# Scoring both attention heads of a pair in one TensorE step, with the transposes grouped, in a hybrid conv/MLA block

## The chip, the cores and the metric

One core of one Trainium2 chip runs the whole program. The metric is the device time of one execution in microseconds; a shorter time is better. The engines of the core run side by side, each with its own queue of instructions in program order: TensorE (PE in the profile, with its weight loads as PEld), VectorE (DVE), ScalarE (ACT), GpSimd (POOL) and SyncE (SP), which issues the DMAs.

## The reference, cut to what matters

```python
D_MODEL, SEQ, CHUNK = 2048, 256, 64
N_HEADS, QK_NOPE, QK_ROPE, V_DIM = 8, 128, 64, 128
...
proj = rms_norm(x) @ w_in                  # u | gate_b | gate_c | c_q | c_kv | k_rope_raw
q  = (rms_norm(c_q)  @ w_uq).reshape(b, s, N_HEADS, QK_NOPE + QK_ROPE)
kv = (rms_norm(c_kv) @ w_ukv).reshape(b, s, N_HEADS, QK_NOPE + V_DIM)
q_rope, k_rope = apply_rope(q_rope), apply_rope(k_rope_raw)      # one k_rope for all heads
for start in range(0, 256, 128):           # two blocks of queries: keys 0..127, keys 0..255
    s = (einsum(q_nope[start:end], k_nope[:end]) + einsum(q_rope[start:end], k_rope[:end])) * scale
    s = where(visible, s, NEG_INF)
    p = softmax(s)
    o = einsum(p, v[:end])
y = concat(short_conv(...), group_rms_norm(o)) @ w_o
x = x + rms_norm(y)
x = x + rms_norm(square(relu(rms_norm(x) @ w_up)) @ w_down)      # d_ff = 8192
```

All inputs, weights and the output are float32. The score of a query and a key is the sum of a 128-long product (the "nope" part) and a 64-long product (the rotary part).

## The kernel before, in words

**The stream.** Every product with a weight matrix is made from a high and a low part of both operands, three matmuls for one (L593, L594, L595: high by high, low by high, high by low), 128x512 outputs for the most part. Two blocks of 128 tokens make six matmuls of one "step" ("mm" in the list of steps). Weights come in "quads" of four chunks of 128 rows (three for the q projection), 1 MB each, by DMA into four slots of `raw`. Two chunks are a half. ScalarE makes the high part of a half (L882, `split_hi`, 128x1024) once TensorE has used the half that was in its place, and VectorE then the low part (L1141, `split_lo`). There are four places for halves (`AHEAD = 4`): when half h has been used, half h+4 is split into its place.

**The order.** `plan()` (L74) writes by hand one list of steps, and every engine runs its own part of each step in that order. While the strips of the input projection that belong to the convolution, and then the output projection, stream through TensorE, a counter `sub` counts the steps, and `between(sub)` (L115) puts the small steps of attention and convolution between them. The eight heads are worked on as four pairs p = 0 to 3. Pair p starts at sub = 16 + 16p: four kv steps at `at` = 0, six steps of q at `at` = 4, and then the list in L131: kT at 6, qT at 7, qrT at 9, the scores of head 0 at 11 and of head 1 at 12, the transposes of the probabilities of head 0 at 13 and of head 1 at 15, the product with v at 18, and the norm and transposes of the output at 20 to 25. Pairs are 16 steps apart, so the kv step of pair p+1 is at `at` = 16 of pair p.

**The small steps on TensorE.** A transpose is a 128x128 matmul against `ident` (`transposes`, L598, L601), four in a row for kT (bank 4) and qT (bank 5), two for qrT, three for the probabilities of each head (bank 5 for head 0, bank 6 for head 1). A scores step (L770) makes, for one head, four float32 products: L783 with q and k transposed (contraction over 128 rows) and L785 with the rotary parts (contraction over 64 rows; head 0 uses partitions 0 to 63, head 1 partitions 64 to 127), first both for the 128 queries that see 128 keys, then both for the 128 queries that see 256 keys. The profile shows each such float32 product as two weight loads and two matmuls; below they are called its two passes. The results of head 0 lie in bank 6 of PSUM, of head 1 in bank 4.

**The other engines.** For a scores step VectorE masks with two memsets, takes the row maxima and scales them (L1246 to L1251); ScalarE then does two exponentials with row sums (L1007). For probsT, VectorE copies head 0's transposes out of bank 5 (L1258) and ScalarE head 1's out of bank 6 (L1014). The kv step of the next pair writes banks 4 and 5, so TensorE waits ahead of it (L662, L663):

```python
pe.wait_ge(probs_ready, 2 * z["p"])
pe.wait_ge(probsT0_ready, z["p"])
```

Of the kernel before, what the change touches and what calls it, by code (L numbers as in the profile page):

```python
# [33 lines left out]
P = 128  # L34
SEQ = 256
# [38 lines left out]
def plan():  # L74
# [40 lines left out]
    def between(sub):  # L115
        if sub == 7:
            steps.extend([("latT", 0, 0), ("latT", 1, 0), ("krT", 0, 0), ("latT", 2, 0)])
        if sub == 10:
            steps.extend([("latT", 3, 0), ("latT", 4, 0)])
        for p in range(PAIRS):  # L120
            at = sub - 16 - 16 * p
            if at == 0:
                n = quad("kv", p=p, nk=4, width=W)
                products(n)
                steps.append(("kv_out", p, n))
            if at == 4:
                for part in range(2):
                    n = quad("q", p=p, part=part, nk=3, width=QW)
                    products(n)
                steps.append(("q_out", p, n))  # L130
            for when, what, h in [(6, "kT", 0), (7, "qT", 0), (9, "qrT", 0), (11, "scores", 0),  # L131
                                  (12, "scores", 1), (13, "probsT", 0), (15, "probsT", 1), (18, "pv", 0),
                                  (20, "o_squares", 0), (21, "o_norm", 0), (25, "oT", 0)]:
                if at == when:
                    steps.append((what, p, h))
        for c in range(4):
            for half, t in [(0, 77 + 6 * c), (1, 98 + 4 * c)]:
                if sub == t:
                    steps.append(("convT", half, c))
                if sub == t + 2:  # L140
                    steps.append(("conv_square", half, c))
                if sub == t + 5:
                    steps.append(("conv_norm", half, c))
# [119 lines left out]
def hybrid_block(nc, t, out):  # L263
# [7 lines left out]
    with ExitStack() as ctx:  # L271
# [314 lines left out]
        def _(pe):  # L586
# [148 lines left out]
            def step(what, a, b):  # L735
# [4 lines left out]
                elif what == "mm_b1":  # L740
                    stream(a, b, [1])
                elif what == "latT":
                    pe.wait_ge(lat_ready, 1)
                    pe.wait_ge(ident_landed, 16)
                    if a >= 3:

                        pe.wait_ge(latT_lo_ready, a - 2)
                    transposes(LAT_BANK[a], [lat[:, tb, lat_cols(a, c):lat_cols(a, c) + P]
                                             for c in range(2) for tb in range(TB)]).then_inc(latT_filled, 1)
                elif what == "krT":  # L750
                    pe.wait_ge(kr_ready, 4)
                    transposes(6, [kr_rot[:, tb].rearrange("p e r -> p (e r)")
                                   for tb in range(TB)]).then_inc(krT_filled, 1)
                elif what == "kT":

                    pe.wait_ge(q_ready, a + 1)
                    pe.wait_ge(kv0_ready, a + 1)
                    pe.wait_ge(kv1_ready, a + 1)
                    transposes(4, [k_sb[:, tb, h] for h in range(2) for tb in range(TB)]).then_inc(kT_filled, 1)
                elif what == "qT":  # L760
                    pe.wait_ge(q_ready, a + 1)
                    transposes(5, [q_sb[:, tb, h * (NOPE + ROPE):h * (NOPE + ROPE) + NOPE]
                                   for h in range(2) for tb in range(TB)]).then_inc(qT_filled, 1)
                elif what == "qrT":
                    pe.wait_ge(q_rope_ready, 4 * (a + 1))

                    pe.wait_ge(kT_ready, a + 1)
                    transposes(4, [qr_rot[:, tb].rearrange("p e r -> p (e r)")
                                   for tb in range(TB)]).then_inc(qrT_filled, 1)
                elif what == "scores":  # L770
                    p, h = a, b
                    pe.wait_ge(kT_ready, p + 1)
                    pe.wait_ge(qT_ready, p + 1)

                    pe.wait_ge(qrT_ready, p + 1)

                    pe.wait_ge(krT_ready, 1)
                    if p and not h:

                        pe.wait_ge(oT_lo_ready, p)  # L780
                    bank, rp = (6, 4)[h], slice(ROPE * h, ROPE * (h + 1))
                    for tb, cols, keys in [(0, slice(0, P), slice(0, P)), (1, slice(P, 3 * P), slice(0, SEQ))]:
                        nc.tensor.matmul(ps[:, bank, cols], qT_sb[:, h, tb * P:(tb + 1) * P], kT_sb[:, h, keys],  # L783
                                         start=True, stop=False)
                        mm = nc.tensor.matmul(ps[:, bank, cols], qrT_sb[rp, tb * P:(tb + 1) * P], krT[rp, keys],  # L785
                                              start=False, stop=True)
                    mm.then_inc(scores_done, 1)
                elif what == "probsT":
                    pe.wait_ge(probs_ready, 2 * a + b + 1)

                    if b == 0:
                        pe.wait_ge(qT_ready, a + 1)
                    transposes((5, 6)[b], [probs[:, b, i * P:(i + 1) * P] for i in range(3)]
                               ).then_inc(probsT_filled, 1)
                elif what == "pv":
                    pe.wait_ge(kv0_ready, a + 1)
                    pe.wait_ge(kv1_ready, a + 1)
                    pe.wait_ge(probsT0_ready, a + 1)

                    pe.wait_ge(probsT1_ready, a + 1)  # L800
                    for h in range(2):
                        o = [ps[:, 6, (2 * h + tb) * P:(2 * h + tb + 1) * P] for tb in range(TB)]
                        v = [v_sb[:, a % 2, tb, h] for tb in range(TB)]
                        nc.tensor.matmul(o[0], probsT[:, h, 0:P], v[0], start=True, stop=True)
                        nc.tensor.matmul(o[1], probsT[:, h, P:2 * P], v[0], start=True, stop=False)
                        mm = nc.tensor.matmul(o[1], probsT[:, h, 2 * P:3 * P], v[1], start=False, stop=True)
                    mm.then_inc(pv_done, 1)
                elif what == "oT":
                    pe.wait_ge(o_normed, a + 1)
                    transposes(6, [o_sb[:, h, tb] for h in range(2) for tb in range(TB)]).then_inc(oT_filled, 1)  # L810
                elif what == "convT":

                    pe.wait_ge(strip_out_dve, a + 1)
                    pe.wait_ge(strip_out_act, (5, 7)[a])
                    if a:

                        pe.wait_ge(oT_lo_ready, PAIRS)
                        if conv_bank(a, b) == conv_bank(0, 0):

                            pe.wait_ge(conv_std_ready, 4)  # L820
                    elif b:

                        pe.wait_ge(conv_std_ready, b)
                    else:
                        pe.wait_ge(latT_lo_ready, 3)
                    transposes(conv_bank(a, b), [s[:, a, tb, b * P:(b + 1) * P] for s in (u_sb, b_sb)
                                                 for tb in range(TB)]).then_inc(convT_filled, 1)
                elif what == "conv_norm":

                    i = 4 * a + b  # L830
                    pe.wait_ge(ones_ready, 1)
                    pe.wait_ge(conv_sq_ready, i + 1)
                    nc.tensor.matmul(ps[:, conv_bank(a, b), 0:SEQ], ones[:], conv_s[:, i % NCONV, :],  # L833
                                     start=True, stop=True).then_inc(conv_sum_done, 1)
                elif what == "hT":
                    if a < X2_DVE:
                        pe.wait_ge(x2_ready, a + 1)
                    else:
                        pe.wait_ge(x2_pool_ready, a - X2_DVE + 1)
                    if a >= 4:  # L840

                        pe.wait_ge(hT_lo_ready, a - 3)
                    transposes(4 + a % 4, [x_res[:, t0 // P, k * P:(k + 1) * P]
                                           for k, tokens, _ in hT_parts(a)
                                           for t0 in range(tokens.start, tokens.stop, P)]).then_inc(hT_filled, 1)
                elif what == "aT":
                    hidden_transposes(a, used=a > 0)
# [758 lines left out]
```

## Time and profile before

| what | value |
|---|---|
| median of 3 runs | 1102.85 us (1102.71 to 1103.09) |
| the profiled execution, its own time | 1102.91 us |
| its span, first to last instruction | 1101.1 us |
| TensorE busy | 1085.3 us (99% of the span) |
| VectorE busy | 666.1 us (60%) |
| ScalarE busy | 512.3 us (47%) |
| GpSimd busy | 98.3 us (9%) |
| granted TensorE clock, mean | 0.996 of 2.4 GHz |
| HBM | 188 GB/s over the span |

"Busy" is the union of the times of an engine's instructions. Matmuls are pipelined: the next one starts before the one before has ended, so the start of one to the start of the next is what one costs. The view called the chain of waits goes back from the last instruction to what released it and gives each piece of time to one instruction; its pieces lie by the ends of instructions and add up, so a delay in front of a matmul is in that matmul's piece. The timeline gives starts and durations, and puts instructions of one line that follow each other on an engine into one row ("x2").

### The profile page before, as it was taken

How to read it: one execution, taken by the hardware profiler on the slowest of the kernel's cores; microseconds unless marked ns; L12 is line 12 of the kernel's file. 1: busy time of each engine (PE TensorE's matmuls, PEld its weight loads, DVE VectorE, ACT ScalarE, POOL GpSimd, SP SyncE). 2: the span in 40 equal slices, each digit the busy share in tenths (PEclk: the TensorE clock that was granted, in tenths of full speed). 3: DMA queues.
4: the chain of work that ended last, by engine and by line, in shares of the span. 5: the costliest groups of instructions: out<-in, count | busy, mean ns of one | idle time of the engine just before them, and what ended most of it. 6: DMA issues, size and time to landing. Idle time of an engine off the chain costs nothing.

```text
span 1101.1 us, 13608 instructions
## 1 busy us (share of the span) xinstructions
PE 1085.3 (99%) x5002; PEld 900.9 (82%) x5002; DVE 666.1 (60%) x707; ACT 512.3 (47%) x654; POOL 98.3 (9%) x108
## 2 busy tenths in 40 slices
PE   8999999999999999999999999999999999999996
PEld 7888788788888788888888888888888888888884
DVE  6465555558985665565565655656546556565566
ACT  6565444445544564444444444444444444434443
POOL 0010120120000440000000000000000000000004
PEclk9999999999999999999999999999999999999998
DMA  9765445453755555565565665656656656566542
GB/s 341 267 211 188 144 158 168 141 193 116 286 202 192 160 183 177 185 195 183 187 190 188 190 190 190 190 177 204 190 190 190 187 190 193 158 207 192 189 171 77
DMA packets 104336, 207.39 MB, mean 188 GB/s; under 512 B 3696, under 2 KB 9456, under 8 KB 103536
## 3 DMA queue, kind: packets, MB, share of 16 engines
q1 hardware_dynamic: 104160, 206.91, 57.9%
q8 instruction: 21, 0.34, 0.1%
q14 instruction: 11, 0.09, 0.0%
q10 hardware_dynamic: 144, 0.04, 0.0%
HBM read 204.84 MB, written 2.10 MB: 188 GB/s over the span
## 4 chain that ended last, share of the span: by engine, by line
PE 95%; DVE 2%; ACT 1%; POOL 1%; issue 1%; DMA 0%; SPq 0%; DVEq 0%; POOLq 0%; ACTq 0%
PE ps L593 30%; PE ps L595 30%; PE ps L594 30%; PE ps L601 3%; DVE w_lo L1141 1%; PE ps L785 1%; PE ps L783 1%; DMA raw<-in_w_in 0%; PE ps L833 0%; DVE xT_lo L1344 0%; ACT a_sb L1103 0%; ACT u_sb L967 0%; DVE acc L1373 0%; DVE x_res L1183 0%; DVE acc L1364 0%
## 5 line engine op out<-in xcount | busy, mean ns | idle before, releaser
L1141 DVE TENSOR_TENSOR w_lo<-raw,w_hi 128x1024 fp32r<-128x1024 f32 (+2 forms) x383 | 471.0, 1237 | 382.5 <-ACT w_hi L882 382.1
L882 ACT ACTIVATE w_hi<-raw 128x1024 fp32r<-128x1024 f32 (+2 forms) x383 | 397.2, 1039 | 488.1 <-PE ps L595 484.4
L593 PE MATMUL ps<-w_hi,xT_hi 128*128 128x512 f32 (+1 forms) x800 | 315.5, 394 | 3.7 <-DVE xT_lo L1204 2.5
L595 PE MATMUL ps<-w_lo,xT_hi 128*128 128x512 f32 (+1 forms) x800 | 309.8, 387 | 0.0
L594 PE MATMUL ps<-w_hi,xT_lo 128*128 128x512 f32 (+1 forms) x800 | 309.4, 387 | 0.0
L593 PE MATMUL ps<-w_hi,yT_hi 128*128 128x512 f32 x672 | 263.3, 392 | 0.0
L595 PE MATMUL ps<-w_lo,yT_hi 128*128 128x512 f32 x672 | 261.9, 390 | 0.0
L594 PE MATMUL ps<-w_hi,yT_lo 128*128 128x512 f32 x672 | 261.7, 389 | 0.0
L593 PEld LDWEIGHTS ps<-w_hi,xT_hi 128*128 128x128 f32 x800 | 150.4, 188 | 36.6 <-issue 4.5
L595 PEld LDWEIGHTS ps<-w_lo,xT_hi 128*128 128x128 f32 x800 | 150.2, 188 | 30.5
L594 PEld LDWEIGHTS ps<-w_hi,xT_lo 128*128 128x128 f32 x800 | 150.5, 188 | 27.8
L595 PEld LDWEIGHTS ps<-w_lo,yT_hi 128*128 128x128 f32 x672 | 126.2, 188 | 26.3
L594 PEld LDWEIGHTS ps<-w_hi,yT_lo 128*128 128x128 f32 x672 | 126.2, 188 | 26.0
L593 PEld LDWEIGHTS ps<-w_hi,yT_hi 128*128 128x128 f32 x672 | 126.2, 188 | 25.9
L1172 DVE TENSOR_TENSOR acc<-acc,ps 128x1024 f32<-128x1024 f32 x62 | 75.7, 1220 | 20.2 <-PE ps L595 19.0
L1454 POOL TENSOR_TENSOR a_sb<-a_sb 128x1024 f32<-128x1024 f32 x16 | 30.3, 1893 | 615.4 <-ACT a_sb L912 615.4
L912 ACT ACTIVATE a_sb<-ps,rstd_x 128x512 f32<-128x512 f32 x32 | 20.2, 684 | 21.6 <-PE ps L595 21.6
L1162 DVE TENSOR_TENSOR yT_lo<-ps,yT_hi 128x512 fp32r<-128x512 f32 x32 | 20.5, 681 | 0.0
L1007 ACT ACTIVATE probs<-ps,neg_max 128x128 f32<-128x128 f32 (+1 forms) x16 | 6.6, 416 | 22.6 <-DVE neg_max L1251 22.6
L918 ACT ACTIVATE yT_hi<-ps 128x512 fp32r<-128x512 f32 x32 | 17.1, 587 | 0.0
L601 PEld LDWEIGHTS ps<-ident,a_sb 128*128 128x128 f32 x128 | 14.9, 140 | 2.1
L601 PE MATMUL ps<-ident,a_sb 128*128 128x128 f32 x128 | 16.6, 273 | 0.0
(143 smaller groups left out, 452.3 us busy)
## 6 DMA issues: line engine op xcount, KB each, us to landing
raw<-in_w_up SPq DMA_DIRECT2D x64, 1024.0 KB, 5.3
raw<-in_w_down SPq DMA_DIRECT2D x64, 1024.0 KB, 5.1
raw<-in_w_in SPq DMA_DIRECT2D x28, 1024.0 KB, 5.2
raw<-in_w_o SPq DMA_DIRECT2D x16, 1024.0 KB, 5.1
raw<-in_w_uq SPq DMA_DIRECT2D x8, 576.0 KB, 3.9
raw<-in_w_ukv SPq DMA_DIRECT2D x4, 1024.0 KB, 5.1
raw<-in_w_in SPq DMA_DIRECT2D x7, 512.0 KB, 8.1
raw<-in_w_in SPq DMA_DIRECT2D x4, 640.0 KB, 8.1
```

Of the source, the lines that this page charges most:

```text
L593: nc.tensor.matmul(dst, x_hi, hi, start=first, stop=False)
L594: nc.tensor.matmul(dst, x_lo, hi, start=False, stop=False)
L595: mm = nc.tensor.matmul(dst, x_hi, lo, start=False, stop=last)
L601: mm = nc.tensor.transpose(ps[:, bank, i * P:(i + 1) * P], src, ident[:])
L783: nc.tensor.matmul(ps[:, bank, cols], qT_sb[:, h, tb * P:(tb + 1) * P], kT_sb[:, h, keys], start=True, stop=False)
L882: nc.scalar.activation(w_hi[:, slot, 0:size], raw[:, raw_slot, first:first + size], ACT.Copy).then_inc(hi_ready, 1)
L912: ins = nc.scalar.activation(a_sb[:, tb], ps[:, bank + tb], ACT.Relu, scale=rstd_x2[:, tb:tb + 1])
L918: ins = nc.scalar.activation(yT_hi[:, at:at + 4, tb * P:(tb + 1) * P], ps[:, 2 + tb].rearrange("p (c t) -> p c t", c=4), ACT.Copy)
L1141: nc.vector.tensor_tensor(w_lo[:, slot, 0:size], raw[:, raw_slot, first:first + size], f32(w_hi[:, slot, 0:size]), ALU.subtract).then_inc( ...
L1162: ins = nc.vector.tensor_tensor(yT_lo[dst], ps[:, 2 + tb].rearrange("p (c t) -> p c t", c=4), f32(yT_hi[dst]), ALU.subtract)
L1172: nc.vector.tensor_tensor(m, m, ps[:, bank:bank + 2], ALU.add).then_inc(acc_added, 1)
L1454: nc.gpsimd.tensor_tensor(a, a, a, ALU.mult).then_inc(a_ready, 1)
```

## The change

In the list of steps, kT moves from `at` 6 to 7, ahead of qT, so that their eight transposes are one block on TensorE; the scores of head 1 move from 12 to 11, and the transposes of head 0's probabilities from 13 to 15, ahead of head 1's. On TensorE the scores of both heads are made in the step of head 0: first the four nope products (head 0, then head 1), then the four rotary products, the two heads one after the other for each block of queries. The step of head 1 has nothing left on TensorE. The other engines' code is as before, in the new order. With `start` only on the first product of a bank, all later ones of the bank go by PSUM's record of what has been written.

```diff
--- before.py
+++ after.py
@@ -128,8 +128,8 @@
                     n = quad("q", p=p, part=part, nk=3, width=QW)
                     products(n)
                 steps.append(("q_out", p, n))
-            for when, what, h in [(6, "kT", 0), (7, "qT", 0), (9, "qrT", 0), (11, "scores", 0),
-                                  (12, "scores", 1), (13, "probsT", 0), (15, "probsT", 1), (18, "pv", 0),
+            for when, what, h in [(7, "kT", 0), (7, "qT", 0), (9, "qrT", 0), (11, "scores", 0),
+                                  (11, "scores", 1), (15, "probsT", 0), (15, "probsT", 1), (18, "pv", 0),
                                   (20, "o_squares", 0), (21, "o_norm", 0), (25, "oT", 0)]:
                 if at == when:
                     steps.append((what, p, h))
@@ -767,24 +767,29 @@
                     pe.wait_ge(kT_ready, a + 1)
                     transposes(4, [qr_rot[:, tb].rearrange("p e r -> p (e r)")
                                    for tb in range(TB)]).then_inc(qrT_filled, 1)
-                elif what == "scores":
-                    p, h = a, b
+                elif what == "scores" and b == 0:
+                    p = a
                     pe.wait_ge(kT_ready, p + 1)
                     pe.wait_ge(qT_ready, p + 1)
 
                     pe.wait_ge(qrT_ready, p + 1)
 
                     pe.wait_ge(krT_ready, 1)
-                    if p and not h:
+                    if p:
 
                         pe.wait_ge(oT_lo_ready, p)
-                    bank, rp = (6, 4)[h], slice(ROPE * h, ROPE * (h + 1))
-                    for tb, cols, keys in [(0, slice(0, P), slice(0, P)), (1, slice(P, 3 * P), slice(0, SEQ))]:
-                        nc.tensor.matmul(ps[:, bank, cols], qT_sb[:, h, tb * P:(tb + 1) * P], kT_sb[:, h, keys],
-                                         start=True, stop=False)
-                        mm = nc.tensor.matmul(ps[:, bank, cols], qrT_sb[rp, tb * P:(tb + 1) * P], krT[rp, keys],
-                                              start=False, stop=True)
-                    mm.then_inc(scores_done, 1)
+                    parts = [(0, slice(0, P), slice(0, P)), (1, slice(P, 3 * P), slice(0, SEQ))]
+                    for h in range(2):
+                        for tb, cols, keys in parts:
+                            nc.tensor.matmul(ps[:, (6, 4)[h], cols], qT_sb[:, h, tb * P:(tb + 1) * P],
+                                             kT_sb[:, h, keys], start=tb == 0, stop=False, skip_group_check=True)
+                    for tb, cols, keys in parts:
+                        for h in range(2):
+                            rp = slice(ROPE * h, ROPE * (h + 1))
+                            mm = nc.tensor.matmul(ps[:, (6, 4)[h], cols], qrT_sb[rp, tb * P:(tb + 1) * P],
+                                                  krT[rp, keys], start=False, stop=True, skip_group_check=True)
+                            if tb:
+                                mm.then_inc(scores_done, 1)
                 elif what == "probsT":
                     pe.wait_ge(probs_ready, 2 * a + b + 1)
```

## Rows read from the trace of the kernel before

**Rows 1.** The page: busy time by engine (part 1), and the chain by engine (part 4).

```profile
PE 1085.3 (99%) x5002; PEld 900.9 (82%) x5002; DVE 666.1 (60%) x707; ACT 512.3 (47%) x654; POOL 98.3 (9%) x108
...
PE 95%; DVE 2%; ACT 1%; POOL 1%; issue 1%; DMA 0%; SPq 0%; DVEq 0%; POOLq 0%; ACTq 0%
```

**Rows 2.** Who waited for whom, 96 to 262 us: total us, times, longest us.

```profile
DVE w_lo L1141 <- ACT w_hi L882: 67.7, 47, 2.1
ACT w_hi L882 <- PE ps L595: 57.1, 44, 3.2
...
PEld ps L785 <- issue: 2.7, 8, 0.3
PEld ps L593 <- issue: 2.6, 8, 0.3
```

**Rows 3.** Chain of waits, head 0 of pair 0: start us, us, what.

```profile
118.76 0.22 PE ps L783 x2
118.98 0.42 PE ps L785 x2
119.40 0.63 PE ps L783 x2
120.03 0.63 PE ps L785 x2
120.66 0.43 PE ps L593
121.09 0.23 PE ps L594
```

**Rows 4.** Stretches of the eight scores blocks, TensorE alone: their sum and mean.

```profile
sum 15.84, PE 15.84; mean PE 1.98
```

**Rows 5.** Chain of waits at other small steps of TensorE.

```profile
110.77 0.44 PE ps L601 x4
...
128.83 0.33 PE ps L601 x3
...
268.57 0.43 PE ps L833 x2
...
412.15 0.87 PE ps L601 x8
```

**Rows 6.** Timeline of weight loads, head 0, pair 0: start us, us.

```profile
118.91 0.29 PEld L785 LDWEIGHTS ps<-krT,qrT_sb 64*128 64x128 f32 x2
...
119.96 0.29 PEld L785 LDWEIGHTS ps<-krT,qrT_sb 64*128 64x128 f32 x2 [0.33 <-issue]
```

**Rows 7.** Timeline of TensorE, pair 0.

```profile
115.63 0.38 PE L601 MATMUL ps<-ident,qr_rot 128*128 128x128 f32 x2
...
127.28 0.40 PE L593 MATMUL ps<-w_hi,xT_hi 128*128 128x512 f32 x1
...
128.66 0.49 PE L601 MATMUL ps<-ident,probs 128*128 128x128 f32 x3
...
130.38 0.39 PE L593 MATMUL ps<-w_hi,yT_hi 128*128 128x512 f32 x1
```

**Rows 8.** Timeline of ScalarE, pair 0.

```profile
121.82 0.37 ACT L1007 ACTIVATE probs<-ps,neg_max 128x128 f32<-128x128 f32 x1 [3.31 <-DVE neg_max L1251]
...
122.62 1.05 ACT L882 ACTIVATE w_hi<-raw 128x1024 fp32r<-128x1024 f32 x1
...
127.48 1.06 ACT L882 ACTIVATE w_hi<-raw 128x1024 fp32r<-128x1024 f32 x1 [0.55 <-PE ps L595]
```

**Rows 9.** Timeline of VectorE, pair 0.

```profile
113.05 0.68 DVE L1235 COPY kT_sb<-ps 128x512 f32<-128x512 f32 x1
...
120.74 0.11 DVE L1246 MEMSET ps<- 64x64 f32 x1 [0.98 <-PE ps L785]
...
126.09 0.56 DVE L1258 COPY probsT_sb<-ps 128x384 f32<-128x384 f32 x1
128.57 1.23 DVE L1141 TENSOR_TENSOR w_lo<-raw,w_hi 128x1024 fp32r<-128x1024 f32 x1 [1.93 <-ACT w_hi L882]
```

## The prediction

> **What bounds the kernel now.** I read the busy times first: TensorE is busy for 99% of the span, the others for 60% and less, and 95% of the chain that ended last is TensorE [rows 1]. So the time is, nearly, the sum of what TensorE's instructions cost one after the other, and a change pays by what it takes out of that queue, as long as no other engine makes TensorE wait. The waits in the attention stretch (96 to 262 us) come next: ScalarE's weight splits wait for TensorE 44 times, VectorE's for ScalarE 47 times; TensorE waits for neither, only its weight loads sit idle, eight times in front of L785 and eight times in front of the first product after it, with no engine named [rows 2]. Then the chain piece by piece, since its pieces are costs that add up. Head 0 of pair 0: nope product on 128 columns 0.22 us, rotary 0.42, nope on 256 columns 0.63, rotary 0.63, and the stream's next product 0.43 where its neighbours take 0.23 [rows 3]. All eight blocks are alike: by starts they last 1.98 us in the mean [rows 4]; the chain puts 1.90 on the four pieces and 0.20 on the delay of the product behind, 2.10 together.
>
> What would these products cost alone? A 128-column transpose costs 0.11 a pass (four 0.44, three 0.33, eight 0.87), the two 256-column passes of L833 0.43 [rows 5]. So two 128-column passes are 0.22, two 256-column ones 0.43, and everything beyond is 0.20 us at each change between 128-row and 64-row products: 0.42 = 0.22 + 0.20; 0.63 = 0.43 + 0.20, twice; 0.43 = 0.23 + 0.20. Four changes in a block. The weight loads show what a change is: the load of the rotary product comes after 0.33 us idle [rows 6], and so do the stream's first loads behind a block, eight times 0.3 [rows 2]. In the plain stream loads run ahead, beside the matmul before; at a change the array first empties, then the load is paid openly.
>
> **The change, part by part.**
> - *Fewer changes of row mode.* Now 8 for a pair (4 in each block). Afterwards four nope products, one change, four rotary products, one change: 2. Six fewer at 0.20 is 1.20 us a pair, 4.8 us for four pairs. The work of the products themselves is the same: eight 128-column passes at 0.11 and eight 256-column ones at 0.215 in a pair.
> - *Neighbours on different rows.* The four rotary products now go head 0 (partitions 0 to 63), head 1 (64 to 127), head 0, head 1, into banks 6, 4, 6, 4. No row of before shows two such neighbours, so I bound it. Upper end of the cost: each change of rows empties the array as a change of mode does, 3 x 0.20 = 0.60 a pair, 2.4 us in all, lost again. Middle: passes simply in series, 0. Lower end: the last pass of one head runs beside the first of the other, at three borders, which saves 0.11 + 0.11 + 0.215 = 0.43 a pair, 1.7 us in all. Between the last two lies a bound from the loads: in rotary mode two loads start 0.11 apart (0.18 long each, 0.29 for both [rows 6]); if loads go one at a time, eight of them need 0.11 each, and a pass starts only when its load is through. Laid out so, the four short passes run in series (0.43), then head 0's two long ones (0.43), head 1's first long one beside the second of these, since its load is through by then, and head 1's second (0.21) alone: 1.07 where series is 1.29. That saves 0.22 a pair, 0.9 us in all. I take this one, because the only rows that lie near are these loads, spaced by 0.11, and nothing in them excludes that halves of the array work side by side. The Trainium skill (TensorE: Matmul & The Clock Gate, Part 3: Packing small matmuls) has it that matmuls on different row groups run concurrently, with starts about 4 ns apart, also that a load overlaps a running matmul where the row groups differ; by that rule this term would be the lower end, 1.7 us. The trace of before can't say.
> - *Grouped transposes.* Eight in a row cost 0.87, twice four 0.88; twice three 0.66, by 0.11 each six are 0.66 [rows 5]. Worth nothing: there is no fee for entering or leaving a block of transposes. The moves of kT and of head 0's probsT cost nothing either, for the reasons under waits.
> - *kT one step later.* VectorE's copy of kT is through at 113.73 in pair 0 [rows 9], though its transposes were done near 111.2 [rows 5], since a split stands in front. Moved behind six more products (1.4 us), they are done at 112.6, still before the copy's turn. TensorE wants the copy at the qrT step, at 115.63 [rows 7]. Cover: 1.9 us.
> - *Both softmaxes behind each other.* VectorE starts on a head 0.15 us after its last product's start-to-start time is over (120.74 [rows 9]), ScalarE's exponentials start 1.08 later and hold it for 0.8 to 0.9 [rows 8]. Head 1's last rotary product now ends at about 118.60 + 2.80, so VectorE has head 0 from 121.1, head 1 from 122.2; ScalarE has head 1 from 123.3 to 124.2. Queued behind that on ScalarE is the split of the half that TensorE has used at 118.60 + 3.00 + 1.39 = 123.0, and behind the split VectorE's low part: 0.9 to 1.0 us late. The low part is there at 124.2 + 1.06 + 1.23 = 126.5. With four places for halves it is wanted three halves later, after 123.0 + 3 x 2.77 + 0.66 = 132.0. Cover 5.5 us; cost nothing. SP's DMA behind that low part also starts 1 us late, four quads ahead of its use; the splits wait for TensorE here, not for a DMA [rows 2]. Nothing.
> - *Head 0's probsT later.* This is the tight one. The kv step of the next pair waits for VectorE's copy of bank 5. Before, that copy stood two steps earlier, at 126.09 [rows 9]. Now it stands behind the split that follows step 29. From the end of that step (127.28 [rows 7]): ScalarE's split starts 0.20 later (127.48 [rows 8]), VectorE's 1.29 later and lasts 1.23 [rows 9], the copy 0.56: done 3.0 to 3.1 us behind the step. TensorE meanwhile does 6 products (1.38), 6 transposes (0.66), 6 products (1.39): it wants the copy after 3.43, its weight load some 0.2 earlier. Cover 0.1 to 0.4 us, in each of three pairs. I cost it at nothing; if the copy were 0.3 us later, it would cost up to 0.9 in all.
>
> Sum: 4.8 + 0.9 = 5.7 us less. Against the profiled execution's 1102.91 (0.06 above the median): 1097.2. The mean granted clock of the execution is 0.996 of 2.4 GHz and TensorE never idles here, so there is no term for the clock.
>
> **The rivals.**
> - *The two heads don't run side by side*: 4.8 only, 1098.1. For it: all rows show passes in series. It is also the case in which the pairing doesn't do what its name says. Chance 0.27.
> - *Full overlap*: 4.8 + 1.7, 1096.4. For it speaks only that loads and matmuls overlap everywhere in the stream; against it the load spacing of 0.11. Chance 0.20. It is what the Trainium skill's page named above would give.
> - *Changing rows costs like changing mode*: 4.8 - 2.4, 1100.5, about 0.2% faster, so half of this counts as no change. The row of the load at the change of mode has both at once, other rows and another mode, and can't tell them apart. Chance 0.10. The Trainium skill (TensorEngine Tiling (Array Packing), Key Properties) says that changing the mode drains TensorE and that another tile of the same mode does not; by it this rival falls. The first half the trace bears out with 0.20 us, the second no row shows.
> - *The kv step waits for head 0's transposed probabilities.* Partly, as above: up to 0.9 back, about 1098. Chance 0.05. On the other side: each pair's kv starts late by what the copy is late beyond its 0.4, three times; the gain of 5.7 is gone at 1.9 us of waiting a pair, which is a copy 2.3 us later than I make it. One more split ahead of it on ScalarE and VectorE (1.06 + 1.23 = 2.3) does just that, and if it is the split behind step 31, which starts only when TensorE is already at the kv step, the wait is 0.2 + 1.1 + 1.2 + 0.56 = 3.1, 9.2 in all: 1102.9 - 5.7 + 9.2 = 1106.4. Against it: in the list the copy stands before that split. Chance of an outcome slower than before by this, or by a delay of this kind that I don't see: 0.04.
>
> **How the numbers follow.** The forecast, overlap limited by loads, has 0.34; with the rivals 0.27, 0.20, 0.10, 0.05 and 0.04. The point is its 1097.2. The range goes from full overlap with 0.5 us for the rounding of the 0.20s (24 changes at up to 0.02 each way) to past the serial case with the small kv wait: 1095.9 to 1099.5; left out are the changing-rows case and the slower one, 0.14, and some tails. A measurement of this kernel can tell about 0.2% (2.2 us) from no change. Faster by more: all up to 1100.6, 0.34 + 0.27 + 0.20 + 0.05 and a part of 0.10 less tails, 0.88. Same 0.08, slower 0.04.
>
> **What the profile after would show.** TensorE still at 99% and the chain as before. In it, pair 0: L783 x8 about 1.30, then L785 with 0.20 in front, then 0.43 for the next product. L785's eight passes are 1.27 to 1.31 in series, 1.07 by the loads, 0.87 in full overlap, 1.9 if rows cost like modes: this one figure decides among four cases. Idle of weight loads in front of L785 falls from eight times to four. L601 costs the same in total. ScalarE's first split after the exponentials starts about 1 us later behind TensorE than now. If the kv product of pairs 1 to 3 stands with "<-DVE probsT_sb L1258" in front of it, the cover was too thin. The prediction is wrong if that wait is over 0.3 us, or if a change of mode in the new block costs other than 0.20.

## The result, and the profile after

| | before | changed |
|---|---|---|
| median | 1102.78 us (4 runs, 1102.71 to 1103.09) | 1095.35 us (4 runs, 1095.19 to 1095.45) |
| profiled execution, its own time | 1102.91 us | 1095.19 us |
| span | 1101.1 us | 1093.4 us |
| TensorE busy | 1085.3 us | 1079.1 us |

The ratio is 0.9932 (95% interval 0.992 to 0.9944): 7.4 us faster, where 5.7 was forecast. The time lies 0.55 us under the low end of the range, 1095.9. On the page TensorE is the bound as before (parts 1 and 4):

```profile
PE 1079.1 (99%) x5002; PEld 898.9 (82%) x5002; DVE 665.4 (61%) x707; ACT 512.3 (47%) x654; POOL 98.3 (9%) x108
...
PE 95%; DVE 2%; ACT 1%; POOL 1%; DMA 1%; issue 0%; SPq 0%; DVEq 0%; POOLq 0%; ACTq 0%
```

The chain of waits through pair 0's scores, now one block (start us, us, what; the eight passes of the nope products are L784 here, those of the rotary products L789):

```profile
118.26 0.23 PE ps L595
118.49 1.31 PE ps L784 x8
119.80 0.86 PE ps L789 x8
120.66 0.43 PE ps L593
121.08 0.23 PE ps L594
```

The nope products take 1.31 as forecast, and the 0.43 of the stream's next product holds one change of row mode. The forecast's deciding figure is the rotary piece: 0.86, which is 0.20 for the change and 0.66 for eight passes. In series they would be 1.3. The forecast's four figures for this stretch (0.87 the lowest, for full overlap) leave out the 0.20, so they are to be set against 0.66, and it lies under all four; that the piece of 0.86 looks like the 0.87 is chance. So a pair's scores cost 1.31 + 0.86 + 0.20 = 2.37 us, against twice 2.10 before [rows 3, 4]: 1.83 less, 7.3 in four pairs, which is the whole gain. (The profiled executions differ by 7.7; 0.3 of that stands ahead of the first scores, which begin at 118.33 instead of 118.60.)

How eight passes fit into 0.66 shows in the timeline, cut to 40 ns and to 20 ns around the first rotary passes (a row counts what has started by the end of the cut):

```profile
119.73 0.38 PE L789 MATMUL ps<-krT,qrT_sb 64*128 64x128 f32 x2
...
119.73 0.49 PE L789 MATMUL ps<-krT,qrT_sb 64*128 64x128 f32 x4
```

Two passes have started by 119.74, four by 119.96. The loads come in twos as well:

```profile
119.73 0.19 PEld L789 LDWEIGHTS ps<-krT,qrT_sb 64*128 64x128 f32 x2 [0.33 <-issue]
```

Two loads of 0.18 us within 0.19, where two of one head took 0.29 [rows 6]. Both heads load and stream at once, from the first pass to the last.

The waits around it (96 to 256 us), to set against [rows 2]: the idle of the weight loads is halved, four times each instead of eight; ScalarE waits for TensorE as before, and no wait of TensorE for VectorE or ScalarE is there.

```profile
ACT w_hi L887 <- PE ps L595: 56.7, 44, 3.2
...
PEld ps L593 <- issue: 1.3, 4, 0.3
PEld ps L789 <- issue: 1.3, 4, 0.3
```

The two covers that I had worked out held. ScalarE's split stands behind both heads' exponentials and starts at 123.67 instead of 122.62 [rows 8], 1.05 us later (0.9 to 1.0 forecast); nothing waited for it:

```profile
123.57 0.20 ACT L1012 ACTIVATION_READ_ACCUMULATOR probs<-ps,neg_max 128x1 f32 x1
123.67 1.05 ACT L887 ACTIVATE w_hi<-raw 128x1024 fp32r<-128x1024 f32 x1
```

VectorE's copy of head 0's transposed probabilities ends at 127.81, and pair 1's kv step starts at 128.21, 0.40 later, as forecast (0.1 to 0.4); ahead of pairs 2 and 3 it is 0.41 and 0.32. VectorE, then TensorE:

```profile
127.26 0.55 DVE L1263 COPY probsT_sb<-ps 128x384 f32<-128x384 f32 x1
```

```profile
126.19 0.82 PE L601 MATMUL ps<-ident,probs 128*128 128x128 f32 x6
...
128.21 0.39 PE L593 MATMUL ps<-w_hi,yT_hi 128*128 128x512 f32 x1
```

### The profile page after: what moved, and what is told of

The parts are those of the page before. It is cut to its first block, busy times and chain, and to the rows that moved or that the text cites. A ratio compares the mean times of both kernels' runs of the same rounds, so it can differ in the third digit from the quotient of the medians.

```text
span 1093.4 us, 13600 instructions
## 1 busy us (share of the span) xinstructions
PE 1079.1 (99%) x5002; PEld 898.9 (82%) x5002; DVE 665.4 (61%) x707; ACT 512.3 (47%) x654; POOL 98.3 (9%) x108
## 4 chain that ended last, share of the span: by engine, by line
PE 95%; DVE 2%; ACT 1%; POOL 1%; DMA 1%; issue 0%; SPq 0%; DVEq 0%; POOLq 0%; ACTq 0%
PE ps L593 30%; PE ps L595 30%; PE ps L594 30%; PE ps L601 3%; DVE w_lo L1146 1%; DMA xT_raw<-in_xT 1%; PE ps L784 0%; PE ps L838 0%; PE ps L789 0%; DVE xT_lo L1349 0%; ACT a_sb L1108 0%; ACT u_sb L972 0%; DVE acc L1378 0%; DVE x_res L1188 0%; DVE acc L1369 0%
## 5 line engine op out<-in xcount | busy, mean ns | idle before, releaser
L595 PE MATMUL ps<-w_lo,cqT_hi 128*128 128x384 f32 x48 | 16.1, 335 | 0.0
```

Of the source, the lines that this page charges most:

```text
L595: mm = nc.tensor.matmul(dst, x_hi, lo, start=False, stop=last)
```

## The experiments

Nine kernels, each against the kernel before on the same chip. The theory after the result: 0.20 us for each change of row mode (24 fewer, 4.8 us), and the two heads' rotary passes wholly beside each other (0.65 us a pair, 2.6 us). The rivals: part of the gain comes from the grouped transposes; the overlap has another cause than the rows; or it hangs on the order of the products. The changed kernel was timed beside other runs of before (median 1102.78) than the experiments were, so a difference against its 1095.35 is good to some 0.3 us; the length of a scores block, the same to 0.01 us in all pairs of a run, is the finer measure.

| run | median us | chain, pair 0: scores pieces |
|---|---|---|
| before | 1102.8 to 1103.0 | 0.22, 0.42, 0.63, 0.63, +0.20, twice |
| changed | 1095.35 | 1.31, 0.86, +0.20 |
| transposes_only | 1102.72 | as before |
| scores_only | 1095.43 | as changed |
| heads_apart_sorted | 1099.87 | 0.66, 0.85, +0.20, twice |
| same_rows | 1097.90 | 1.31, 1.50, +0.20 |
| four_changes | 1096.89 | 0.44, 0.42, 1.06, 0.63, +0.20 |
| full_rows | 1096.33 | 1.31, 1.31, +0 |
| head_by_head | 1095.26 | 1.31, 0.86, +0.20 |
| rotary_twice | 1098.88 | 1.31, 1.61, +0.20 |
| twice_head_by_head | 1100.33 | 1.31, 2.06, +0.20 |

**Which half of the edit pays.** transposes_only changes the list alone, from the kernel before:

```diff
-            for when, what, h in [(6, "kT", 0), (7, "qT", 0), (9, "qrT", 0), (11, "scores", 0),
-                                  (12, "scores", 1), (13, "probsT", 0), (15, "probsT", 1), (18, "pv", 0),
+            for when, what, h in [(7, "kT", 0), (7, "qT", 0), (9, "qrT", 0), (11, "scores", 0),
+                                  (12, "scores", 1), (15, "probsT", 0), (15, "probsT", 1), (18, "pv", 0),
```

> Only the list is changed: kT at 7 and head 0's probsT at 15; the scores are made as before, head by head. Theory (transposes have no fee for entering or leaving a block, and VectorE's copy for the kv step comes in time): 1102.8, within 0.3 us of before. Rival (a part of the gain of 7.4 us comes from the grouping, since 4.8 + 1.7 us is all that I had for the scores): 1 us or more below before. Rival (kv step waits for head 0's copy): up to 1 us above before, with that wait named at L593.

Measured: 1102.72 against 1102.92, ratio 0.9997 (0.9988 to 1.0007). Nothing.

scores_only is the changed kernel with kT at 6 and head 0's probsT at 13:

```diff
-            for when, what, h in [(7, "kT", 0), (7, "qT", 0), (9, "qrT", 0), (11, "scores", 0),
-                                  (11, "scores", 1), (15, "probsT", 0), (15, "probsT", 1), (18, "pv", 0),
+            for when, what, h in [(6, "kT", 0), (7, "qT", 0), (9, "qrT", 0), (11, "scores", 0),
+                                  (11, "scores", 1), (13, "probsT", 0), (15, "probsT", 1), (18, "pv", 0),
```

> The scores are made as in the changed kernel, both heads in one step; kT stays at 6 and head 0's probsT at 13, so no transposes are grouped. Theory (all of the gain is in the scores blocks): 1095.4, as the changed kernel within 0.3 us. Rival (grouping matters): 1096.4 or more.

Measured: 1095.43, ratio 0.9931 (0.9914 to 0.9947), the same as the changed kernel's. All of the gain is in the scores.

**The changes of row mode alone.** heads_apart_sorted, from the kernel before, sorts the products within a head and leaves the heads apart:

```diff
-                    for tb, cols, keys in [(0, slice(0, P), slice(0, P)), (1, slice(P, 3 * P), slice(0, SEQ))]:
+                    parts = [(0, slice(0, P), slice(0, P)), (1, slice(P, 3 * P), slice(0, SEQ))]
+                    for tb, cols, keys in parts:
                         nc.tensor.matmul(ps[:, bank, cols], qT_sb[:, h, tb * P:(tb + 1) * P], kT_sb[:, h, keys],
-                                         start=True, stop=False)
+                                         start=tb == 0, stop=False, skip_group_check=True)
+                    for tb, cols, keys in parts:
                         mm = nc.tensor.matmul(ps[:, bank, cols], qrT_sb[rp, tb * P:(tb + 1) * P], krT[rp, keys],
-                                              start=False, stop=True)
+                                              start=False, stop=True, skip_group_check=True)
```

> The heads stay in steps of their own, at 11 and 12, but each makes its two nope products first and then its two rotary ones: 4 changes of row mode in a pair instead of 8, no two heads side by side. Theory (0.20 us for each change, passes of one head in series): 16 changes fewer, 3.2 us: 1099.6, each block 1.70 us in the chain. Rival (a change costs little, and the gain comes from overlap): 1101.5 or more.

Measured: 1099.87, ratio 0.9973 (0.9962 to 0.9983), 3.05 us under before for 16 changes: 0.19 each. The chain at head 0:

```profile
118.59 0.66 PE ps L784 x4
119.25 0.85 PE ps L787 x4
120.10 0.43 PE ps L593
```

**The rows alone.** same_rows, from the changed kernel, moves head 1's rotary products onto head 0's partitions (head 1 gets head 0's rotary part):

```diff
-                            rp = slice(ROPE * h, ROPE * (h + 1))
+                            rp = slice(0, ROPE)
                             mm = nc.tensor.matmul(ps[:, (6, 4)[h], cols], qrT_sb[rp, tb * P:(tb + 1) * P],
```

> The changed kernel, but the rotary products of both heads read partitions 0 to 63, so both use the same rows of the array; head 1's scores get head 0's rotary part. Changes of mode, banks and order are as in the changed kernel. Theory (the eight passes overlap by pairs only because the heads lie on different rows): the rotary stretch takes 0.20 + 1.29 us instead of 0.86, so 0.63 us more in each pair, 2.5 in all: 1097.9. Rival (the rows don't matter, other banks or the grouping make them fast): 1095.4.

Measured: 1097.90, ratio 0.9955 (0.9938 to 0.9971), 2.55 us over the changed kernel. The chain:

```profile
118.78 1.31 PE ps L784 x8
120.09 1.50 PE ps L789 x8
121.59 0.43 PE ps L593
```

1.50 for 0.86, with banks, order and changes of mode kept. So the heads run side by side because they lie on different rows of the array (rows and the partitions that they are read from go together and can't be told apart), and this is worth 0.64 us a pair. It is also, to 0.2 us, the 1098.1 of my serial rival.

**More changes, overlap kept.** four_changes, from the changed kernel:

```diff
-                    for h in range(2):
-                        for tb, cols, keys in parts:
+                    for tb, cols, keys in parts:
+                        for h in range(2):
                             nc.tensor.matmul(ps[:, (6, 4)[h], cols], qT_sb[:, h, tb * P:(tb + 1) * P],
                                              kT_sb[:, h, keys], start=tb == 0, stop=False, skip_group_check=True)
-                    for tb, cols, keys in parts:
                         for h in range(2):
```

> The changed kernel, but in each pair nope and rotary products alternate by block of queries: nope, nope (128 keys), rotary pair, nope, nope (256 keys), rotary pair. The rotary pairs are side by side as before, the changes of row mode are 4 in a pair instead of 2. Theory (0.20 us each, overlap whole in each pair of neighbours): 8 changes more, 1.6 us: 1097.0. Rival (a change between short blocks costs less, or overlap needs the longer block): under 1096.2, or over 1098.

Measured: 1096.89, ratio 0.9944 (0.9928 to 0.9961), 1.54 us over the changed kernel for 8 changes: 0.19 each again. The pieces are the short pair 0.42 (0.20 + 0.22) and the long one 0.63 (0.20 + 0.43): each pair takes the time of one head.

```profile
118.67 0.44 PE ps L784 x4
119.12 0.42 PE ps L788 x4
119.54 1.06 PE ps L784 x4
120.60 0.63 PE ps L788 x4
121.23 0.43 PE ps L593
```

**No change of mode at all.** full_rows, from the changed kernel, with the sum of both heads' rotary parts in each head's scores:

```diff
-                            rp = slice(ROPE * h, ROPE * (h + 1))
+                            rp = slice(0, P)
                             mm = nc.tensor.matmul(ps[:, (6, 4)[h], cols], qrT_sb[rp, tb * P:(tb + 1) * P],
```

> The changed kernel, but the rotary products take all 128 partitions (each head's scores get the sum of both heads' rotary parts): no change of row mode at all, and no overlap. This is what rotary operands padded with zeros would cost. Theory (0.20 us for a change, overlap worth 0.65 us a pair): 0.65 - 0.40 = 0.25 us more in a pair, 1.0 in all: 1096.4. Rival (the change of mode isn't what costs 0.20 us, another kind of border is): 1097.5 or more.

Measured: 1096.33, ratio 0.9939 (0.9922 to 0.9955), 1.0 us over the changed kernel.

```profile
118.80 1.31 PE ps L784 x8
120.11 1.31 PE ps L789 x8
121.42 0.23 PE ps L593
```

Both fees of 0.20 are gone, on the way in and on the way out, and with them the overlap. The fee belongs to the change between 128 and 64 rows and to nothing else at these borders. The starts in the changed kernel split it in two: the first rotary load and pass start 0.09 us after the last nope pass has had its 0.22 (119.42 + 0.22 = 119.64, against 119.73), and the same half's second pass follows 0.21 behind the first (119.94) instead of 0.11. That the array empties in the first part and a weight load stands in the open in the second is how I read it; no run takes them apart.

**The order.** head_by_head, from the changed kernel:

```diff
-                    for tb, cols, keys in parts:
-                        for h in range(2):
+                    for h in range(2):
+                        for tb, cols, keys in parts:
                             rp = slice(ROPE * h, ROPE * (h + 1))
```

> The changed kernel, but the four rotary products go head 0, head 0, head 1, head 1, so that only the middle two are neighbours on different rows. Theory A (products start in program order, and one on the other rows runs beside the one that still runs): head 0's short one alone, head 0's long one with head 1's short one, then head 1's long one alone, 0.20 us more in a pair, 0.9 in all: 1096.2. Theory B (each half of the rows has a queue of its own): no change, 1095.4. Theory C (the one on record, loads one at a time and passes in order): 1.07 + 0.20 us for the rotary stretch, 1.7 in all: 1097.0.

Measured: 1095.26, ratio 0.9935 (0.9918 to 0.9952): no change. The times of A and B are only 0.8 us apart, so the chain has to decide between them: its rotary piece is 0.86, where A would make it some 1.07 and C 1.27. With two products of head 0 (four passes) issued ahead of head 1's first, two passes had still started by 119.52:

```profile
119.50 0.39 PE L789 MATMUL ps<-krT,qrT_sb 64*128 64x128 f32 x2
```

Of which head they are, the shapes tell. In program order two passes of 128 columns and two of 256 (head 0) stand ahead of head 1's first of 128; by 119.84 all four of 128 have started and only one of 256:

```profile
L789 PE MATMUL ps<-krT,qrT_sb x5: 272/373/378, 119.5 to 119.8; 64*128 64x128 f32 x4, 64*128 64x256 f32 x1
```

Theories A and C fall, B stands: a half of the rows doesn't wait for products of the other half that were issued before.

rotary_twice, from the changed kernel, counts the rotary part double:

```diff
                             rp = slice(ROPE * h, ROPE * (h + 1))
+                            nc.tensor.matmul(ps[:, (6, 4)[h], cols], qrT_sb[rp, tb * P:(tb + 1) * P],
+                                             krT[rp, keys], start=False, stop=False, skip_group_check=True)
                             mm = nc.tensor.matmul(ps[:, (6, 4)[h], cols], qrT_sb[rp, tb * P:(tb + 1) * P],
```

> The changed kernel with each rotary product issued twice in a row (the rotary part counts double in the scores). Program order is then head 0, head 0, head 1, head 1 for each block of queries. Theory A (order of starts kept, other rows side by side): for each block of queries head 0's first product alone, then its second beside head 1's first, and so on; with short ones 0.22 and long ones 0.43 the eight products take about 0.22 + 0.22 + 0.43 + 0.43 + 0.43 = 1.73 us against 0.65, 1.1 a pair, 4.3 in all: 1099.7. Theory B (a queue for each half): 1.30 us, 0.65 more a pair, 2.6 in all: 1098.0. Series would be 1.94 a pair more than the pairs side by side, 7.8 in all: 1103.1.

Measured: 1098.88, ratio 0.9961 (0.9947 to 0.9975), 3.5 us over the changed kernel, midway between B (2.6) and A (4.3). The chain accounts for 3.0 of it, 0.75 a pair, 0.1 more than B has; the other 0.5 stands outside the scores blocks, about the size of the scatter of these runs (1098.39 to 1099.51). The chain says where it is off:

```profile
121.14 0.43 PE ps L789 x4
121.57 0.22 PE ps L791 x4
121.80 0.53 PE ps L789 x4
122.32 0.43 PE ps L791 x4
122.76 0.43 PE ps L593
```

Short passes in twos at full overlap (0.20 + 0.22, then 0.22), the last four too (0.43), but 0.53 in the first long ones, 0.1 too many: one half paid a weight load in the open (the first load for one half's long passes starts at 121.51, 0.11 ahead of its pass, for the other half only at 121.63, with its pass). B without a limit doesn't explain that; a queue of a half that holds only so much, behind which the common order waits, would. Its depth is what the last run asks for.

twice_head_by_head is rotary_twice with the loops swapped as in head_by_head:

```diff
-                    for tb, cols, keys in parts:
-                        for h in range(2):
+                    for h in range(2):
+                        for tb, cols, keys in parts:
                             rp = slice(ROPE * h, ROPE * (h + 1))
```

> Each rotary product twice, as in rotary_twice, but all four of head 0 first and then all four of head 1: eight passes of one half of the rows stand ahead of the other half's first. Theory (each half has a queue of its own that holds about four passes, and what comes behind a full queue waits in program order; in rotary_twice head 1's first long product got its load only when head 0's long one started): head 1 starts when head 0's fifth pass starts, 0.43 us behind it, then needs 1.29 and a load in the open of 0.1: a scores block of about 3.5 us against 3.1 in rotary_twice, 1100.1 in all. Rival 1 (the queue of a half is deeper): head 1 starts within 0.05 us of head 0, block 3.0, 1098.0. Rival 2 (products start in program order, one next to the other): 3.9, 1101.4.

Measured: 1100.33, ratio 0.9977 (0.9967 to 0.9986). The timeline of TensorE and of its loads from the first rotary pass on, cut at 121.41:

```profile
120.84 0.48 PE L789 MATMUL ps<-krT,qrT_sb 64*128 64x128 f32 x2
121.17 0.38 PE L791 MATMUL ps<-krT,qrT_sb 64*128 64x128 f32 x2
121.39 0.38 PE L789 MATMUL ps<-krT,qrT_sb 64*128 64x256 f32 x2
```

```profile
120.84 0.29 PEld L789 LDWEIGHTS ps<-krT,qrT_sb 64*128 64x128 f32 x2 [0.33 <-issue]
121.06 0.30 PEld L791 LDWEIGHTS ps<-krT,qrT_sb 64*128 64x128 f32 x2
121.28 0.30 PEld L789 LDWEIGHTS ps<-krT,qrT_sb 64*128 64x128 f32 x3
```

Head 0's four short passes run alone. With its fifth pass, its first long one at 121.39, another pass and another load start within 0.02. It is head 1's, since that pass has 128 columns and head 0's four of these had started (L789 alone, 121.34 to 121.40):

```profile
L789 PE MATMUL ps<-krT,qrT_sb x2: 373/376/378, 121.4 to 121.4; 64*128 64x256 f32 x1, 64*128 64x128 f32 x1
```

The chain's rotary pieces (0.42, 0.22, 0.33, 0.22, 0.22, 0.09, 0.12, 0.43) go from 120.91 to 122.97, 2.06, so the block is 1.31 + 2.06 + 0.20 = 3.57 us, where the theory had about 3.5, a deeper queue 3.0 and program order 3.9. So four passes of one half stand in its queue, the one that has just started among them; a fifth, and all that is issued behind it, waits. A rival that I had not put up is one look-ahead over the common order, with a fixed reach. It doesn't fit this trace: head 1's first pass, ninth in the order, waited for the fifth, four places ahead of it, while head 1's third, the eleventh, started at 121.72 with the seventh, four places ahead too, not started before 121.83. The timeline of 121.60 to 121.80:

```profile
121.72 0.27 PE L791 MATMUL ps<-krT,qrT_sb 64*128 64x128 f32 x1
```

## Why the prediction was right and wrong

- *TensorE's queue is the time; no other engine comes in.* Right. Nothing waited at the kv step, the cover was 0.40 us, the late split cost nothing.
- *0.20 us for each change of row mode, 24 fewer, 4.8 us.* Right: 0.19 in heads_apart_sorted and in four_changes, 0 in full_rows, and same_rows, which has this gain alone, stands at 1097.90 for a forecast 1098.1. TensorEngine Tiling (Array Packing) in the Trainium skill, Key Properties, names a drain at a change of tiling mode, and none for another tile of the same mode. The runs agree with both: 0.20 for the change, and no gap between neighbours on different rows (in full_rows, without a change of mode, the 0.20 is gone).
- *Grouped transposes, moved steps: nothing.* Right, 0.9997 in transposes_only.
- *Neighbours on different rows: 0.9 us, with 1.7 as the lower end of the cost.* This step failed, and it is why the time fell out of the range. It measured 2.55 us (same_rows against the changed kernel), 0.64 a pair in the chain. Two assumptions went in. First, loads one at a time, 0.11 apart: the row that I took it from has two loads of the same half [rows 6], and it says nothing of two halves; after the change two loads of different halves start within 0.01 us. Second, and in both ends of my bound, that the two passes of a product hold back what is issued behind them, so that only border passes could run side by side. They don't: head 1's first pass runs beside head 0's first. So my rival of full overlap (1096.4) was too slow as well. The true lower end was half the time of the series, 0.65 a pair, 2.6 us. With it the sum is 4.8 + 2.6 = 7.4, which is what was measured.
- *The page of the Trainium skill that spoke for full overlap* (TensorE: Matmul & The Clock Gate, Part 3: Packing small matmuls) was the better guide: concurrent matmuls on different row groups, starts some 4 ns apart. Here they are 0.01 us apart, and I had turned its rule into my own too narrow "border passes" before giving it a time. Its sentence that matmuls start strictly in program order doesn't hold here: in head_by_head head 1's first pass, with four passes of head 0 ahead of it in the program, started at 119.52, ahead of all but the first of them, with no loss.
- *Slower than before, and changed rows at the cost of a changed mode:* nothing of either was seen.

## What to carry to other kernels

Where TensorE is the bound, sort small products by how many rows they contract over, so that each change between 128 and 64 rows (0.20 us here) is paid once for many. Put 64-row products of independent work on different halves of the partitions and into different banks: two then cost what one does. If an operand can be padded with zeros to 128 rows instead, weigh 2 x 0.20 us of changes against the lost overlap: here padding loses by 0.25 us a pair, and for a single pair of short products, which saves 0.22 us by overlap and pays 0.40, it should win, by the same numbers (not run).

## What the runs showed of the hardware that I had not expected

Each half of the array's rows behaves as if it took loads and passes from a queue of its own. Two halves start within 0.02 us of each other even when four passes of one were issued first (head_by_head), and it makes no difference to the time. The queue holds four passes, the one that has just started among them: with eight issued first, the other half started with the fifth, 0.55 us after the first (twice_head_by_head, 120.84 to 121.39), and in rotary_twice one half's fifth pass got its load only when the other half's fifth had started (121.63 and 121.62), as it would by the same rule. So the order of products matters only when more than four passes of one half stand together. Whether two halves may also write the same bank at once was not tried; the heads wrote to banks 6 and 4 in every run. One thing follows that no run tested: since a pass issued later on the other half can start first, a signal on the last product issued doesn't say that the earlier ones are through. In the changed kernel both heads add to one counter, `scores_done`, and their last passes start 0.01 us apart; that head 0 is done first rests on both halves having the same passes to do.
